# Applying the input norm's gain to the weight rows at their split instead of to x

## What is computed

```
def _rmsnorm(x, g):
    xf = x.astype(jnp.float32)
    y = xf * lax.rsqrt(jnp.mean(xf * xf, axis=-1, keepdims=True) + EPS)
    return (y * g.astype(jnp.float32)).astype(x.dtype)

h = _rmsnorm(x, g)                       # x (1088, 2048), g (2048,)
proj = h @ w_in                          # w_in (2048, 6152)
u, z_ssm, q, k, v, z_att, f_pre = jnp.split(proj, splits, axis=-1)
y_ssm = _s5_scan(u, ...)                 # complex diagonal state space, 64 groups of 16 channels
zs = jax.nn.gelu(y_ssm, approximate=False)
y_ssm = zs * sigmoid(zs @ w_glu + b_glu) * silu(z_ssm), then _rmsnorm
y_att = forgetting attention of 8 heads on q, k, v, f_pre, times silu(z_att), then _rmsnorm
x = x + concatenate([y_ssm, y_att]) @ w_out
```

## Time and profile before

| | us |
|---|---|
| median of 3 runs | 1929.95 (1927.86 to 1930.5) |
| the profiled execution | 1928.19 |
| its span in the trace | 1926.6 |
| TensorE busy in it | 1896.8 |
| VectorE, ScalarE, GpSimd busy | 1137.6, 709.2, 441.0 |

### The profile page before, as it was taken

One profiled execution on the slowest core, in us unless ns is written; L12 is line 12 of the kernel. 1 busy time (PEld: TensorE's weight loads), 2 busy tenths in 40 slices (PEclk: granted clock), 3 DMA queues, 4 the chain that ended last, 5 costly groups with the idle time before them and its releaser, 6 DMA issues.

```text
span 1926.6 us, 32969 instructions
## 1 busy us (share of the span) xinstructions
PE 1896.8 (98%) x11368; PEld 1773.8 (92%) x11368; DVE 1137.6 (59%) x2189; ACT 709.2 (37%) x1395; POOL 441.0 (23%) x756
## 2 busy tenths in 40 slices
PE   5999999999999999999999999999999999999999
PEld 4899999999999999999999999999999997888877
DVE  7865665556455564545645456455566566776664
ACT  6422333333243334333343333343345443333341
POOL 5874445556112002020020200202002010100121
PEclk9999999999999999999999999999999999999999
DMA  9343343444325224132141321423338454432573
GB/s 226 105 119 108 109 109 101 120 127 123 93 74 168 84 60 143 54 108 79 55 149 57 105 80 55 139 68 94 93 99 276 153 200 139 133 122 98 180 257 122
DMA packets 212055, 230.50 MB, mean 120 GB/s; under 512 B 33978, under 2 KB 167188, under 8 KB 210772
## 3 DMA queue, kind: packets, MB, share of 16 engines
q1 hardware_dynamic: 185392, 143.58, 26.5%
q0 software_dynamic: 21072, 74.93, 11.7%
q10 hardware_dynamic: 5524, 11.14, 1.6%
HBM read 166.83 MB, written 62.74 MB: 119 GB/s over the span
## 4 chain that ended last, share of the span: by engine, by line
PE 94%; DVE 4%; DMA 1%; issue 0%; ACT 0%; SPq 0%; POOL 0%; POOLq 0%; DVEq 0%; ACTq 0%
PE GB L195 61%; PE TB L2350 3%; PE TB L2482 3%; PE TB L2483 3%; PE TB L2484 3%; PE TB L2371 3%; PE GB L2482 2%; PE GB L2483 2%; PE GB L2484 2%; PE TB L2392 2%; PE TB L1137 1%; PE TB L1147 1%; PE TB L1148 1%; PE TB L2411 1%; DVE XL L673 1%; PE TB L2336 0%
## 5 line engine op out<-in xcount | busy, mean ns | idle before, releaser
L195 PE MATMUL GB<-XH,whi 128*128 128x384 f32 x2448 | 827.6, 338 | 1.0 <-ACT QR L1740 0.8
L195 PE MATMUL GB<-XH,wlo 128*128 128x384 f32 x2448 | 800.5, 327 | 0.0
L195 PE MATMUL GB<-XL,whi 128*128 128x384 f32 x2448 | 798.0, 326 | 0.0
L195 PEld LDWEIGHTS GB<-XH,whi 128*128 128x128 f32 x2448 | 459.9, 188 | 14.2 <-issue 8.9
L183 DVE TENSOR_TENSOR wlo<-wraw,whi 128x256 fp32r<-128x256 f32 x412 | 201.9, 493 | 456.4 <-ACT whi L179 451.3
L195 PEld LDWEIGHTS GB<-XL,whi 128*128 128x128 f32 x2448 | 460.2, 188 | 5.3 <-issue 3.8
L195 PEld LDWEIGHTS GB<-XH,wlo 128*128 128x128 f32 x2448 | 459.3, 188 | 0.0
L179 ACT CAST whi<-wraw 128x256 fp32r<-128x256 f32 x412 | 166.5, 405 | 644.8 <-PE GB L195 634.3
L2089 DVE RECIPROCAL SQ<-SQ 128x136 f32<-128x136 f32 x128 | 127.7, 997 | 1.4
L1787 ACT ACTIVATE PR<-PR,nmx 128x128 f32<-128x128 f32 (+8 forms) x72 | 53.4, 742 | 184.4 <-DVE nmx L2060 171.8
L1545 POOL DMA_DIRECT2D t_s<-TS x16 | 11.7, 733 | 360.9 <-DVE TS L1978 311.7
(11 more groups left out here) (517 smaller groups left out, 2877.2 us busy)
## 6 DMA issues: line engine op xcount, KB each, us to landing
wraw<-in_w_in SPq DMA_DIRECT2D x380, 128.0 KB, 2.2
TS<-in_w_out POOLq DMA_DIRECT2D x32, 512.0 KB, 5.6
t_s<-TS POOLq DMA_DIRECT2D x16, 1024.0 KB, 4.8
AREA<-in_w_out SPq DMA_DIRECT2D x34, 256.0 KB, 3.2
AREA<-in_x_prompt POOLq DMA_DIRECT2D x32, 256.0 KB, 4.8
AREA<-t_s SPq DMA_DIRECT2D x30, 256.0 KB, 2.7
out_y_prompt<-AREA POOLq DMA_DIRECT2D x28, 256.0 KB, 3.1
xt<-in_x_prompt SPq DMA_DIRECT2D x5, 1024.0 KB, 5.4
```

The source lines that it names most:

```text
L195: ins = T.matmul(group(GB if bank is None else bank, b), w[:, s % SPL, kk], x[:, k + kk, c:c + n], start=first and kk == 0 and i == 0, sto ...
```

## The change

The gain leaves x. `x_scale` multiplies a tile by its token factor alone, one `tensor_scalar` over all 2048 columns. The gain is loaded as 16 more rows of `vin` on ScalarE's queue, transposed with the others and lies in `vec[:, 34:50]`, one column for each block of 128 rows. The two broadcast loads on SP are gone. Each piece of `w_in` is now split block by block: ScalarE copies with a per-partition scale (`gain * w`, rounded), VectorE computes `gain * w - high` in one `scalar_tensor_tensor`; two instructions of 128 columns on each engine in place of one of 256. The eight pieces of the first tile are split in the same way; the gate columns `wf` are multiplied by the gain on VectorE once, before their split. The pieces of `w_glu` keep the single operation (`k=None`).

```diff
@@ class Weights
-            def split_hi(self, m, s, loads):
+            def split_hi(self, m, s, loads, k=None):
                 S.wait_ge(self.w_in[s % RAW], 16 * (self.turns + loads))
                 S.wait_ge(self.mm, self.base + m + 1)
+                if k is not None:
+                    for kk in range(PIECE):
+                        ins = S.activation(whi[:, s % SPL, kk], wraw[:, s % RAW, kk], ACT.Copy, scale=gain[:, k + kk:k + kk + 1])
+                    ins.then_inc(self.hi, 1)
+                    return
                 S.copy(whi[:, s % SPL], wraw[:, s % RAW]).then_inc(self.hi, 1)
-            def split_lo(self, m, s):
+            def split_lo(self, m, s, k=None):
                 V.wait_ge(self.hi, self.base + m + 1)
+                if k is not None:
+                    for kk in range(PIECE):
+                        ins = V.scalar_tensor_tensor(wlo[:, s % SPL, kk], wraw[:, s % RAW, kk], gain[:, k + kk:k + kk + 1],
+                                                     whi[:, s % SPL, kk].bitcast(f32), ALU.mult, ALU.subtract)
+                    ins.then_inc(self.lo, 1)
+                    return
@@ sync
-                for i in range(2):
-                    sp.dma_start(gain[i], norm_gain[0:1, :].to_broadcast([P, D_MODEL]).rearrange("p (k h c) -> p h k c", k=KT, h=2)[:, i]
-                                 ).then_inc(ld_gain, 16)
@@ scalar
+                act.dma_start(vin[34:34 + KT], row128(norm_gain)).then_inc(ld_par, 16)
...
-                        act.wait_ge(ld_wf, 16)
+                        act.wait_ge(wg_in, 1)
                         S.copy(wg[:, :, 0:NH], wf).then_inc(wg_hi, 1)
...
                         for p in range(SPL):
-                            S.copy(uhi[:, p], uraw[:, p]).then_inc(W.hi, 1)
+                            for kk in range(PIECE):
+                                k = HP + PIECE * p + kk
+                                ins = S.activation(uhi[:, p, kk], uraw[:, p, kk], ACT.Copy, scale=gain[:, k:k + 1])
+                            ins.then_inc(W.hi, 1)
@@ x_scale
-                    if m == 0:
-                        dve.wait_ge(ld_gain, 32)
-                    for b in range(2):
-                        x = x_all(m)[:, :, 64 * b:64 * (b + 1)]
-                        ins = V.scalar_tensor_tensor(x, x, y, gain[b][0:n], ALU.mult, ALU.mult)
-                    ins.then_inc(xs_done, 1)
+                    V.tensor_scalar(x_all(m), x_all(m), y, None, ALU.mult).then_inc(xs_done, 1)
@@ vector
-                V.tensor_copy(vec[:], GB[:, 0:34]).then_inc(par_ev, 1)
+                V.tensor_copy(vec[:], GB[:, 0:34 + KT]).then_inc(par_ev, 1)
                 V.tensor_copy(prm[:].rearrange("p a b -> p (a b)"), GB[:, 64:224]).then_inc(par_ev, 1)
+                dve.wait_ge(par_ev, 1)
+                dve.wait_ge(ld_wf, 16)
+                V.tensor_tensor(wf, wf, gain.unsqueeze(2).to_broadcast([P, KT, NH]), ALU.mult).then_inc(wg_in, 1)
@@ attention
+            def split_k(last, m):
+
+                return None if last and m >= NPC else PIECE * (m % 8)
...
-                            W.split_lo(h * NPC + m, m)
+                            W.split_lo(h * NPC + m, m, split_k(last, m))
```

More of the change, by code:

```diff
@@ L128, in build_kernel @@
         delta = sb("delta", [P, GC])
-        vec = sb("vec", [P, 34])
+        vec = sb("vec", [P, 34 + KT])
+        gain = vec[:, 34:34 + KT]
         epsc = sb("epsc", [P, 1])
@@ L246, in build_kernel @@
             cin = XLF[:, :, 7 * P:8 * P]
-            gain = [a[:, :, 8 * P:TOK] for a in (XHF, XLF)]
             fold = [XLF[:, 2 * i:2 * i + 2, 5 * P:6 * P] for i in range(2)]
@@ L282, in build_kernel @@
         ld_x = [sem(f"ld_x{m}") for m in range(TT)]
-        ld_gain, ld_u, ld_par, ld_b, ld_c, st_pk, ld_wf = (
-            sem(n) for n in ("ld_gain", "ld_u", "ld_par", "ld_b", "ld_c", "st_pk", "ld_wf"))
+        wg_in, ld_u, ld_par, ld_b, ld_c, st_pk, ld_wf = (
+            sem(n) for n in ("wg_in", "ld_u", "ld_par", "ld_b", "ld_c", "st_pk", "ld_wf"))
         ident_done, par_t, par_ev, dt_bc = sem("ident_done"), sem("par_t"), sem("par_ev"), sem("dt_bc")
@@ L520, in scalar @@
                         for p in range(SPL):
-                            W.split_hi(p, p, 1)
+                            W.split_hi(p, p, 1, PIECE * p)
                     if m == 3:
@@ L586, in body @@
                                 S.activation(cols(zs, b), group(GB, b), ACT.Silu).then_inc(e["ga"], 1)
-                        W.split_hi(m + SPL, s + SPL, turn(j, s + SPL) if s + SPL < NPC else turn(j, s) + 1)
+                        W.split_hi(m + SPL, s + SPL, turn(j, s + SPL) if s + SPL < NPC else turn(j, s) + 1,
+                                   PIECE * ((s + SPL) % HP))
                         if s in at["table"]:
@@ L628, in scalar @@
                 for s in range(SPL):
-                    W.split_hi(HP + s, s, turn(0, s))
+                    W.split_hi(HP + s, s, turn(0, s), PIECE * s)
                 act.wait_ge(st_pk, 16)
@@ L691, in vector @@
                         dve.wait_ge(wg_hi, 1)
+                        dve.wait_ge(wg_in, 1)
                         V.tensor_tensor(wg[:, :, NH:2 * NH], wf, wg[:, :, 0:NH].bitcast(f32), ALU.subtract).then_inc(wg_lo, 1)
@@ L694, in vector @@
                         for p in range(SPL):
-                            W.split_lo(p, p)
+                            W.split_lo(p, p, PIECE * p)
                         dve.wait_ge(den_in, 1)
@@ L708, in vector @@
                             dve.wait_ge(W.hi, SPL + p + 1)
-                            V.tensor_tensor(ulo[:, p], uraw[:, p], uhi[:, p].bitcast(f32), ALU.subtract).then_inc(W.lo, 1)
+                            for kk in range(PIECE):
+                                k = HP + PIECE * p + kk
+                                ins = V.scalar_tensor_tensor(ulo[:, p, kk], uraw[:, p, kk], gain[:, k:k + 1], uhi[:, p, kk].bitcast(f32),
+                                                             ALU.mult, ALU.subtract)
+                            ins.then_inc(W.lo, 1)
                 o = Order(dve, "dve_ssm")
@@ L769, in body @@
                             rest_u(j + 1, m, j)
-                        W.split_lo(m + SPL, s + SPL)
+                        W.split_lo(m + SPL, s + SPL, PIECE * ((s + SPL) % HP))
                         if s == at["k"]:
@@ L832, in vector @@
                 for s in range(SPL):
-                    W.split_lo(HP + s, s)
+                    W.split_lo(HP + s, s, PIECE * s)
                 dve.wait_ge(W.mm, W.multiplied(HP - 1))
@@ L1014, in tensor @@
                 pe.wait_ge(ident_done, 2)
-                pe.wait_ge(ld_par, 16 * 11)
+                pe.wait_ge(ld_par, 16 * 12)
                 pe.wait_ge(dt_bc, 1)
-                T.transpose(GB[:, 0:34], vin, ident[0:34, 0:34])
+                T.transpose(GB[:, 0:34 + KT], vin, ident[0:34 + KT, 0:34 + KT])
                 for i in range(5):
@@ L1759, in part @@
                             m = s + SPL
-                            W.split_hi(h * NPC + m, m, h * (NPC // RAW) + m // RAW + 1)
+                            W.split_hi(h * NPC + m, m, h * (NPC // RAW) + m // RAW + 1, split_k(last, m))
                             if not att:
```

6 lines of the change are left out of this document (3 added, 3 removed).

## The result

| | us |
|---|---|
| kernel before, median | 1930.22 (1927.86 to 1931.87, 4 runs) |
| changed kernel, median | 1952.28 (1949.05 to 1952.6, 4 runs) |
| ratio | 1.0116, 95% interval 1.0104 to 1.0128 |
| spans of the profiled executions | 1926.6 and 1950.5 |

The change makes the kernel 22 us slower. I had forecast 12 us, with a range that ended at 1950: the sign was right, and the time lies outside the range. The experiments show that the forecast sum was nearly complete (a version of the changed kernel without the thing I had missed takes 1941.7 us, with errors of up to 0.9 us in single terms that partly cancel), and that the rest comes from something that no term of it held: VectorE must fetch its own code again.

What follows compares the result with a forecast made beforehand. VectorE, fed by DMA, was taken to bound the start and TensorE the rest. Terms -4.8 + 5.0 + 0.5 + 11.1 + 0.7 = +12.5 on 1928.2, plus 1.8 for the median, gave 1942.4 us; eight-in-ten range 1932 to 1950.

Steps and rivals of the forecast that it cites:

- What bounds the kernel: Before 50 us VectorE, fed by DMA; behind it TensorE alone, with delays counting where TensorE arrives just as VectorE finishes.
- The price of the pair: Two split operations of 128 columns end after 0.70 us on ScalarE (0.30 later) and 0.61 on VectorE (0.18 later).
- upper ends: Split delays of 0.30 us on ScalarE and 0.18 on VectorE, chosen over lower bounds of 0.10 and 0.06.
- the rival of the cheap halves: Weight splits: scale operand costs nothing, step 0.16 us, 0.06 where busy; total 1930, no change; chance 0.13.
- The start, -4.8: Before 50 us: removed broadcast loads and faster x scaling win 4.8 us net of added splits; ends -2 and -7.
- The passes, 7 x 0.72: Seven state-space passes: four splits in VectorE's gapless chain to the third u bank's copy delay TensorE, +5.0 us in all.
- The last pass, +0.5: Last state-space pass: three splits in the chain to its y product, for which TensorE already waits, +0.5 us.
- The heads, 7 x 1.58: Seven heads with attention: delays of 0.48, 0.45, 0.29 and 0.36 us in slots 4, 6, 9 and 16, +11.1 us.
- The first head, +0.7: First head: only the sums of squares, twice, with no margin, 0.48 + 0.18 us.
- GpSimd case: Passes: one more half falls behind GpSimd's scan product, +2 to 4 us, 1947 to 1950 with a poor start; chance 0.25.
- the start decides: Loops hide all split delays since pieces are split four ahead, only the start's gain remains: 1925 us; chance 0.07.
- What was to show it: Signs: halves near 400 and 350 ns, x scaling 1.3 us, sixth transposes near 45, named gaps grown, head 122.9 us.

Runs made afterwards that it cites:

- e8: Changed kernel with 60 empty instructions at VectorE's very start, so that its loop over heads lies on words 521-818: 1941.69 us (ratio 1.0063).
- e7: Changed kernel without gain in the weight pieces, each piece of w_in split in two plain operations on both engines, VectorE's code moved: 1930.31 us.
- e4: Changed kernel with every split in one operation and the gain left out of the weight pieces: 1923.46 us (ratio 0.9970).
- e12: Changed kernel, code moved, VectorE's low parts put behind other work in the heads (last: to slot 19) and behind the third bank's copy in passes: 1927.55 us.
- e1: Changed kernel with 60 more one-word instructions on VectorE in the first head, moving the loop body to words 521-818: 1943.17 us (ratio 1.0067).
- e10: Changed kernel, code moved by 72 words, VectorE's low part behind the slot's other work in the heads with attention: 1937.06 us (ratio 1.0042).
- e14: Kernel before with 32 empty instructions in VectorE's loop body and 317 at its very start, body on words 717-1014: 1960.97 us, one run.
- e11: Kernel before with VectorE's low part behind the slot's other work in the heads with attention, nothing else: 1936.52 us (ratio 1.0027).

## Why the prediction was right and wrong

- **What bounds the kernel**: right. TensorE's waits after the change are for VectorE at the named places.
- **The price of the pair**: right. 0.70 us on ScalarE and 0.61 on VectorE were forecast, 0.70 and 0.61 measured (medians over the 380 pairs of e8). Taking the upper ends, since they came from the same operations, was the right choice; the rival of the cheap halves is what e7 shows for operations without the operand, 6.8 us, and not for these.
- **The start, -4.8**: right, as far as one start can be told from another. At its end (row 4) the changed kernel is 4.2 us ahead, e8 5.5, and e4, without the halves, 6.6: the halves of the first tile cost 1.1 to 2.4, and I had allowed 1.4. Which part of the gain is the loads' and which VectorE's is not shown.
- **The passes, 7 x 0.72**: 0.58 each. Mechanism right, size a little high, and e12 shows that two thirds of it follow the splits in the chain as I put it. The last pass, +0.5, was right (0.6).
- **The heads, 7 x 1.58**: 1.62 in e8 for each of the six heads of the loop, with loads idle in slots 4, 6, 9 and 16 for 0.75, 0.46, 0.34 and 0.49. Right. The last head costs 2.3 us, since there a fifth place waits (0.29 and 0.65 for the copies in two slots instead of 0.49 in one); mis-sized by 0.7.
- **The first head, +0.7**: 1.5 (1.6 in e8). The first squares wait 0.85 us instead of 0.37, as forecast; the second 1.81 instead of 0.76, which is 1.05 more and not 0.18. Ahead of them VectorE is busy without a gap from a split that waits for ScalarE (at 562.91 in the kernel before), and three more splits follow: 0.48 + 3 x 0.18 = 1.02.
- **The step that failed** stands in no line of the sum. I costed instructions by their duration and by who stands behind them, and took for granted that their number has no price of its own: the body of VectorE's loop over heads grew from 266 to 298 words, and 61 more stood ahead of it. That cost 8 us at five jumps (9 to 11 by the medians of e1 and e8). It is also why the range was too narrow: its upper end was made of the GpSimd case, and I gave no chance to anything that comes of longer code. By the rule of the experiments it could have been counted: of the 256 places in a block where a body can begin, it reaches into three blocks from 9 with 266 words, and from 41 with 298.
- **The rivals**: "the start decides" fell, the gaps grew where I said. "GpSimd gets between the halves", my case for a time near 1950, did not come: the passes cost less than forecast, not more. That the time came out near its number is no credit to it.
- **What was to show it**: all of the list came (395 and 348 ns, a scaling of 1.3 us, slots 4 and 6, the third bank with 0.64 us on the loads, transposes of the sixth tile at 46.31) but one: a head takes 124.0 us where it has a fetch (the first of them 126.6), and 122.9 as forecast where it has none.

## What to carry to other kernels

Doubling the instructions of a small operation that runs ahead of every slot's work costs what the engine's next dependent work is late, not the operation's own length: look for the places where the bounding engine arrives just as the other finishes, price those, and put the small operation behind them if its buffers leave it time, and if nothing that is awaited stands in the DMA queue behind the load that refills them (e10). A factor from SBUF is not free in an operation of 128 columns: here it cost more than splitting the operation did. And when a loop's body grows past 256 instructions (here seen on VectorE alone), count it and see where it lies: an "issue" idle time right behind the jump back means a fetch, and a few dozen empty instructions ahead of the loop, at a place where the engine waits anyway, can take it away.

## What the hardware showed that I had not expected

- VectorE's code is fetched again at a loop's jump back if the body lies badly: five times 3.5 to 7 us on top of its normal idle time, in words 461 to 758 and 717 to 1014, and never 20 to 60 words further on. The DMA queue of instructions carries 55 to 57 packets then, otherwise 30 to 32.
- An empty instruction on VectorE takes about 0.1 us: 317 of them put its first operation at 31.65 us.
- After a gap of 2.22 us in TensorE's loads the granted clock was 0.50 for 3.4 us; after gaps of 1.0 us it stayed at 1.00, but also after one of 2.24 in e14 and one of 3.66 in e10.
- A scale from SBUF costs ScalarE 99 ns in a copy of 128 columns (395 in the changed kernel against 296 in e7).
- A low part made later in the slot delays SP's later loads: those of `XLF` by 6.3 us in e11.
